# mLSTM decay rows, gate tiles and convolution taps in a new order, and GLA heads in turn, in a two-block float32 kernel

## The reference, cut to what matters

```
h      = rms_norm(x, g) * (1 + sc) + sh              # (512, 1024)
p      = split(h @ w_in)                             # ml_q .. ml_f, gla_q .. gla_a, conf, sc, gate
# mLSTM, 4 heads of 64; with b = cumsum(log_sigmoid(f)) and m the running maximum of (i - b):
qk[t,s] = (q_t . k_s / 8) * exp(i_s - b_s - m_t)     for s <= t, else 0
h_t     = sum_s qk[t,s] v_s / max(|sum_s qk[t,s]|, exp(-(b_t + m_t)))
y_ml    = (head_rms_norm(h_t) * sigmoid(ml_o)) @ w_ml_out
# conformer: 31 causal taps over 256 channels, then layer norm, silu, projection
u      = layer_norm(dwconv31(a * sigmoid(g)));  y_conf = silu(u) @ w_conf_out + b
# GLA, 4 heads of 64, chunks of 16: o = (masked q k) v inside a chunk + q . state before it
merged = g0 * y_ml + g1 * y_gla + g2 * y_conf + g3 * y_sc;   block output = merged @ w_o
```

## Time and profile before

| | |
|---|---|
| median of three executions | 1870.16 us |
| span of the profiled execution, first to last instruction | 1862.2 us |
| what lies around the span (median less span) | 8.0 us |
| mean granted clock of TensorE | 0.944 |
| PE busy | 1752.2 us, 94% |
| DVE / ACT / POOL busy | 900.6 / 662.8 / 421.5 us |
| chain that ended last | PE 81%, DVE 12%, waiting for nothing shown 2%, ACT 2% |

### The profile page before, as it was taken

One profiled execution on the slowest core, in us unless ns is written; L12 is line 12 of the kernel. 1 busy time (PEld: TensorE's weight loads), 2 busy tenths in 40 slices (PEclk: granted clock), 3 DMA queues, 4 the chain that ended last, 5 costly groups with the idle time before them and its releaser, 6 DMA issues.

```text
span 1862.2 us, 20099 instructions
## 1 busy us (share of the span) xinstructions
PE 1752.2 (94%) x7716; PEld 1379.7 (74%) x7716; DVE 900.6 (48%) x1193; ACT 662.8 (36%) x794; POOL 421.5 (23%) x152
## 2 busy tenths in 40 slices
PE   6897999999998979999999799999998999999997
PEld 4676667877877748888888478777767688888886
DVE  4559215332789464444433375385444244444323
ACT  2341215323313254454322432243343355454222
POOL 0347202411433401111100045533203211111000
PEclk8898779977999989999999999999999999999999
DMA  8231202210656213333322122222202233332321
GB/s 291 77 93 46 67 24 68 91 46 23 218 176 216 70 44 100 103 90 90 113 90 91 62 68 91 75 69 70 66 24 68 79 91 90 93 109 90 113 90 45
DMA packets 190956, 168.60 MB, mean 91 GB/s; under 512 B 9157, under 2 KB 180717, under 8 KB 190765
## 3 DMA queue, kind: packets, MB, share of 16 engines
q1 hardware_dynamic: 173485, 148.49, 25.9%
q10 hardware_dynamic: 16800, 16.83, 2.8%
q0 software_dynamic: 608, 2.41, 0.3%
HBM read 165.61 MB, written 2.10 MB: 90 GB/s over the span
## 4 chain that ended last, share of the span: by engine, by line
PE 81%; DVE 12%; issue 2%; ACT 2%; SPq 1%; DMA 1%; POOL 0%; DVEq 0%; ACTq 0%
PE bank L1091 22%; PE bank L1093 22%; PE bank L1092 22%; DVE work L1564 4%; DVE work L1627 2%; PE bank L1173 2%; PE bank L1316 1%; DVE tbuf L1536 1%; PE bank L1116 1%; DVE h_lo L1542 1%; SPq L235 1%; PE bank L1236 1%; PE bank L1449 1%; PE bank L1157 1%; PE bank L1227 1%
## 5 line engine op out<-in xcount | busy, mean ns | idle before, releaser
L1091 PE MATMUL bank<-h_hi,w_hi 128*128 128x512 f32 x1536 | 617.0, 402 | 30.1 <-DVE h_lo L1542 23.9
L1092 PE MATMUL bank<-h_lo,w_hi 128*128 128x512 f32 x1536 | 605.8, 394 | 0.0
L1093 PE MATMUL bank<-h_hi,w_lo 128*128 128x512 f32 x1536 | 605.5, 394 | 0.0
L573 POOL TENSOR_TENSOR w_lo<-w_raw,w_hi 128x2048 fp32r<-128x2048 f32 x63 | 326.1, 5177 | 551.9 <-ACT w_hi L648 551.7
L1091 PEld LDWEIGHTS bank<-h_hi,w_hi 128*128 128x128 f32 x1536 | 293.6, 191 | 114.7 <-issue 35.4
L648 ACT ACTIVATE w_hi<-w_raw 128x2048 fp32r<-128x2048 f32 x131 | 250.3, 1911 | 311.1 <-PE bank L1093 241.0
L1093 PEld LDWEIGHTS bank<-h_hi,w_lo 128*128 128x128 f32 x1536 | 293.2, 191 | 62.6
L1092 PEld LDWEIGHTS bank<-h_lo,w_hi 128*128 128x128 f32 x1536 | 293.9, 191 | 60.5 <-issue 1.7
L1524 DVE TENSOR_TENSOR w_lo<-w_raw,w_hi 128x2048 fp32r<-128x2048 f32 x68 | 156.8, 2306 | 252.5 <-ACT w_hi L648 252.5
L1091 PE MATMUL bank<-y_hi,w_hi 128*128 128x512 f32 x480 | 192.1, 400 | 11.2 <-DVE tbuf L1747 8.4
L1897 DVE SCALAR_TENSOR_TENSOR work<-bank,par,work 128x510 f32<-128x510 f32 (+1 forms) x176 | 123.5, 744 | 142.1 <-ACT work L933 142.1
(11 more groups left out here) (223 smaller groups left out, 1534.4 us busy)
## 6 DMA issues: line engine op xcount, KB each, us to landing
w_raw<-in_w_in SPq DMA_DIRECT2D x94, 512.0 KB, 4.6
w_raw<-in_ffn_w_up SPq DMA_DIRECT2D x44, 512.0 KB, 4.6
w_raw<-in_w_up SPq DMA_DIRECT2D x44, 512.0 KB, 4.6
work<-in_ada_w ACTq DMA_DIRECT2D x16, 1024.0 KB, 7.5
w_raw<-in_ffn_w_down SPq DMA_DIRECT2D x22, 512.0 KB, 4.0
w_raw<-in_w_down SPq DMA_DIRECT2D x22, 512.0 KB, 3.7
work<-in_ada_w SPq DMA_DIRECT2D x8, 1024.0 KB, 12.1
w_raw<-in_w_o SPq DMA_DIRECT2D x8, 512.0 KB, 4.1
```

The costliest lines, as they stand in the source:

```text
L573: pool.tensor_tensor(w_lo[u % 2][:, :], raw[u % 2][:, :], w_hi[u % 2][:, :].bitcast(FP32), ALU.subtract)\
L1091: pe.matmul(dst, w_hi[s][:, at:at + n], hi, start=first, stop=False)
L1092: pe.matmul(dst, w_hi[s][:, at:at + n], lo, start=False, stop=False)
L1093: return pe.matmul(dst, w_lo[s][:, at:at + n], hi, start=False, stop=last)
```

## The change

What it does:

- **Row broadcast once per head.** `ml_spread(h)` spreads -m over all 512 queries once (4 matmuls in place of 16), into bank 3 or 7. DVE adds the mask of all four diagonal blocks in one instruction (`ml_mask`), and the 16 mask matmuls go. ACT now takes the exponential in two instructions, the diagonal block from what DVE wrote and the rest from the bank.
- **Heads in pairs.** The 16 (head, block) pairs become 8 steps; each does the scores of heads h and h + 1 for one block.
- **Gate tiles in halves.** Each step holds one gate3 tile, 12 matmuls and 12 matmuls (`column_part`), with the spread of heads 2 and 3 (step 3) and the outputs of heads 0 and 1 (step 4) between the halves. The gate2 tile in `gla_result` is halved too.
- **Taps.** The conformer's mean moves from ahead of the mLSTM into step 3, its variance into step 5. The taps are spread from before the gate rows to step 2.
- **Low parts.** Those of the four mLSTM units, the four of gate3 and of y3 move from POOL to DVE, between the taps and in steps 0, 2, 4 and 6.
- **Output turn later.** The turn of the mLSTM output moves from ahead of y3 to after the first GLA unit, and what follows it on ACT and DVE too.
- **GLA.** Both heads' scores come first, then half a tile, head 2c within, half a tile, head 2c + 1 within, and `gla_before` alternates the two heads matmul by matmul.
- The value rows have 66 columns per head in place of 65.

The core of the diff (places in `work` and table entries left out):

```diff
-            for u in range(U["gate2"] + 1):
+            for u in range(IFA + 1):
+                lo(u)
+            for u in range(U["y3"] + 1, U["gate2"] + 1):
                 lo(u)
...
+            def ml_decay(h, j, n):
+                g = ml_gt[:, j * MH + h:j * MH + h + 1]
+                if n >= 2:
+                    wait_read(act, T["ml_qk"][n - 2])
+                act.wait_ge(sem("ml_masked"), h + 1)
+                ins = act.activation(tbuf[:, n % 2, 0:P], ml_masked[:, h % 2, j * P:(j + 1) * P], ACT.Exp, bias=g)
+                if j < TT - 1:
+                    ins = act.activation(tbuf[:, n % 2, P:S - j * P], bank[T["ml_d"][h].bank][:, (j + 1) * P:S], ACT.Exp, bias=g)
+                ins.then_inc(sem("ml_exp"), 1)
...
+            def column_part(name, n, k0, k1):
+                u, t, at = U[name] + n // 2, T[name][n], n % 2
+                if k0 == 0:
+                    weights_ready(u)
+                    wait_free(pe, t)
+                for k in range(k0, k1):
+                    mm = three(bank[t.bank][:, :], u, k * 256 + at * P, P, h_hi[:, k, :], h_lo[:, k, :], k == 0, k == KT - 1)
+                if k1 == KT:
+                    done(mm, t)
...
-            for n in range(MH * TT):
-                h, j = divmod(n, TT)
-                if n == CF_VAR_AT:
-                    conformer_mean(T["cf_var"][0], cf_s, sem("cf_sq"))
-                ml_scores(h, j)
-                if h and j == 1:
-                    ml_values(h - 1)
-                if n in GATE3_AFTER:
-                    column_tile("gate3", GATE3_AFTER[n])
-            ml_values(MH - 1)
-            for cc in (6, 7):
-                column_tile("gate3", cc)
+            for h in range(2):
+                ml_spread(h)
+            for step, (h, j) in enumerate(ML_STEPS):
+                if step == CF_MEAN_AT:
+                    conformer_mean(T["cf_mu"][0], cf_acc, sem("cf_conv"))
+                if step == CF_VAR_AT:
+                    conformer_mean(T["cf_var"][0], cf_s, sem("cf_sq"))
+                for hh in range(2):
+                    ml_scores(h + hh, j, 2 * step + hh)
+                column_part("gate3", step, 0, 4)
+                if step == VALUES_AT - 1:
+                    for hh in range(2):
+                        ml_spread(2 + hh)
+                if step == VALUES_AT:
+                    for hh in range(2):
+                        ml_values(hh)
+                column_part("gate3", step, 4, KT)
+            for hh in range(2):
+                ml_values(2 + hh)
...
             def gla_result(c, tile):
                 gla_scores(2 * c)
-                column_tile("gate2", tile)
+                gla_scores(2 * c + 1)
+                column_part("gate2", tile, 0, 4)
                 wait_free(pe, T["gl_o"][c])
                 gla_within(2 * c)
-                gla_scores(2 * c + 1)
-                gla_before(2 * c)
+                column_part("gate2", tile, 4, KT)
                 gla_within(2 * c + 1)
-                done(gla_before(2 * c + 1), T["gl_o"][c])
+                done(gla_before(c), T["gl_o"][c])
...
-            conf_taps(1, TAPS_FIRST)
+            lo(U["ml"])
+            conf_taps(1, 6)
+            lo(U["ml"] + 1)
...
-            conf_taps(TAPS_FIRST, CONF_W)
+            conf_taps(6, 11)
+            lo(U["ml"] + 2)
+            conf_taps(11, 16)
+            lo(U["ml"] + 3)
+            conf_taps(16, 20)
...
+            def ml_mask(h):
+                t = T["ml_d"][h]
+                wait_full(dve, t)
+                if h >= 2:
+                    dve.wait_ge(sem("ml_exp"), 2 * TT - 1 + h % 2)
+                dve.tensor_tensor(ml_masked[:, h % 2, :].rearrange("p (j t) -> p j t", j=TT), bank[t.bank][:, :].rearrange("p (j t) -> p j t", j=TT),
+                                  const("causal_st").unsqueeze(1).broadcast_to([P, TT, P]), ALU.add).then_inc(sem("ml_masked"), 1)
```

More of the change, by code:

```diff
@@ L395, in program @@
         take("gl_z", AUX, MT)
+        take("ml_hT", AUX, MT)
         take("gl_kdT", AUX, MT)
@@ L735, in _ @@
             log_and_exp()
+            split(U["ml"] + 1)
             t = T["ifa"][0]
@@ L794, in _ @@
             act.activation(ml_ms, ml_ms, ACT.Exp, scale=-0.5).then_inc(sem("ml_rs"), 1)
-            for cc in (6, 7):
-                raw_gate("gate3", cc, 3 * KT)
-            open_gates("gate3")
-            split(U["y3"] + 1)
-            act.wait_ge(w_used, U["y3"] + 1)
-            for k in range(2):
-                y_split(ml_q[:, k, :], k, 3 + k)
             u = U["gla"]
@@ L816, in _ @@
             split(u + 2)
+            for k in range(2):
+                y_split(ml_q[:, k, :], k, 3 + k)
+            act.wait_ge(sem("y_lo"), 6)
             for c in range(2):
@@ L1271, in _ @@
                 (token_unit if k == 2 else column_unit)(U["gla"] + k, T["gla"][2 * k:2 * k + 2])
+                if k == 0:
+                    pe.wait_ge(sem("ml_normed"), 1)
+                    for c in range(MT):
+                        turn(T["ml_hT"][c], [(i * P, ml_h[:, i, c * P:(c + 1) * P]) for i in range(TT)])
             for c in range(MT):
@@ L1704, in _ @@
-            ml_divide(MH - 1)
+            for step, (h, j) in enumerate(ML_STEPS):
+                if step == VALUES_AT + 1:
+                    for hh in range(2):
+                        ml_divide(hh)
+                for hh in range(2):
+                    ml_weights(h + hh, j, 2 * step + hh)
+                if step % 2 == 0:
+                    lo(U["gate3"] + step // 2 + 1)
+                if step < CF_MEAN_AT:
+                    conf_taps(25 + 2 * step, 27 + 2 * step)
+                if step == CF_MEAN_AT - 1:
+                    dve.wait_ge(ch.sem, ch.n)
+                    for c in range(2):
+                        dve.nop().then_inc(sem("cf_conv"), 1)
+                if step == CF_MEAN_AT:
+                    conf_center()
+                    for hh in range(2):
+                        ml_mask(2 + hh)
+                if step == CF_VAR_AT + 1:
+                    wait_read(dve, T["cf_var"][0])
+                    for c in range(2):
+                        dve.scalar_tensor_tensor(out=cf_acc[:, c, :], in0=cf_acc[:, c, :], scalar=col("conf_ln_g", c), in1=rstd[:, :],
+                                                 op0=ALU.mult, op1=ALU.mult).then_inc(sem("cf_scaled"), 1)
@@ L1705, in _ @@
+            for hh in range(2):
+                ml_divide(2 + hh)
             for h in range(MH):
@@ L1769, in _ @@
                                   ALU.subtract).then_inc(sem("gl_bs"), 1)
+            for c in range(MT):
+                t = T["ml_hT"][c]
+                wait_full(dve, t)
+                wait_read(dve, T["ml"][6 + c])
+                release(dve.scalar_tensor_tensor(out=ml_q[:, c, :], in0=bank[t.bank][:, :], scalar=col("ml_norm_g", c), in1=ml_o[:, c, :],
+                                                 op0=ALU.mult, op1=ALU.mult), t)
+                wait_read(dve, t)
+                dve.nop().then_inc(sem("y_src"), 1)
+            for k in range(2):
+                y_lo_of(ml_q[:, k, :], k, 5 + k)
             for c in range(2):
```

195 lines of the change are left out of this document (89 added, 106 removed).

## The result

The changed kernel takes **1802.8 us** (median of four executions, 1801.3 to 1804.5), the kernel before in the same comparison 1869.4: a ratio of 0.9641, 95% interval [0.9627, 0.9655], 66.6 us less. The profiled execution has a span of 1801.8 us and a total of 1804.5. The forecast was 1807, the range 1797 to 1828.

The account below looks back on a forecast made before the run. PE was taken to bound the mLSTM stretch, full of small work at mean clock 0.77. 52.3 us saved up to the GLA projections plus 11.1 in the GLA made 63.4 off 1870.2, rounded 1807 us; range 1797 to 1828.

Parts of the forecast that it names:

- Up to the first spread: Stretch before the mLSTM's first spread: DVE's low parts and taps set the pace, first spread issued at 173.8 us.
- From there to y3: First spread to y3 on PE: 68.8 us work, 2.6 waits, 2.5 half clock, together 73.9; y3 starts at 247.7.
- the one of step 5: Second score of step 5 waits 1.0 us for the bank DVE frees at the end of two divides.
- the fifth tile: In y3: 0.4 us lost because DVE frees this tile's bank late, after its divides and squares.
- The GLA: State matmuls with alternating heads at 0.065 us a record, 8.1 us per pair; 11.1 us saved over both pairs.
- The tiny turn at 0.074: Eight tiny matmuls at the mLSTM's turn, 0.074 us each, taken as the dearest that issuing alone can be.
- Sum: Whole kernel: 52.3 us by the GLA projections plus 11.1 in the GLA, 63.4 off the span, 1862.2 to 1798.8.
- The median stands 8.0 above the span, and I keep that: Step from span to time: 1870.2 - 63.4, rounded, gives 1807 us.
- GLA gains nothing: Rival for the GLA heads: a fixed cost per instruction, the 11.1 us fall to about 0, 1818 us; chance 0.20.
- Clock not won back: Rival, first spread to y3: mean clock stays 0.77, 93 us in place of 73.9, 1826 us; chance 0.11.
- DVE becomes the bound: Rival: nine low parts moved to DVE make step 3's mean wait some 20 us, 1827 us; chance 0.08.
- Slower through the weight buffers: Rival: late low parts delay reloads, nine units showing 8.8 us each, 79 us, giving 1886 us; chance 0.02.

Follow-up runs that it names:

- run 3: Changed kernel with the first GLA unit's low part on DVE, after its fourth y3 tile, in place of POOL: 1795.5 us.
- run 5: Changed kernel with the first GLA unit's low part on DVE and, for the second GLA pair, DVE's masked copies ahead of scan and norm: 1788.4 us.
- run 8: Kernel before with the GLA part of the change alone: 1855.3 us against 1867.0, ratio 0.9925.
- run 11: Kernel before, unchanged, profiled again: span 1860.2 us, total 1862.0.
- run 1: Changed kernel with the state matmuls of the two GLA heads one head after the other again: 1814.7 us.
- run 6: Changed kernel with 16 spreads and 16 mask matmuls put back on PE as idle work, overwritten by the scores: 1838.8 us.
- run 7: Changed kernel with the nine low parts of the mLSTM, gate3 and y3 units back on POOL: 1811.1 us.
- run 10: Changed kernel with two idle spreads (4 records, about 1.9 us) on PE ahead of the first spread: 1806.5 us.

## Why the prediction was right, and where it was not

**Up to the first spread.** Forecast 173.8, came at 172.4. DVE's first low part ends at 125.1 as forecast, PE waits 1.7 and not 2.0 for the token unit. The rest is a half-clock stretch of the kernel before in this place (clock 0.97 against 1.00), which I had not counted as a gain.

**From there to y3.** Forecast 73.9, measured 71.5. Spreads 3.8 against 4.4, because two neighbouring ones cost 1.9 together; scores 5.9 against 5.8, so the second head is free as the score rows said; values 0.115 us each at full clock (40 in 4.58) against 0.113; waits 1.8 against 2.6, the one of step 5 did not come; one half-clock stretch, at the values, of two allowed. y3 starts at 243.8 in place of 247.7.

**y3: the step that failed.** I allowed 0.4 us for the fifth tile, "whose bank DVE frees late". It was about 6 (y3 took 17.35 us, against 11.55 in run 3 at full clock): 3.57 of wait and the half clock behind it. The cause, shown by run 3, is POOL's low part of the first GLA unit. It was not among the nine that moved, so I did not follow it; but ACT's split before it is tied to the end of gate3, which now falls together with DVE's last divides. I had named the mutual hold as something that ends and did not ask where the low parts left on POOL would meet DVE next.

**The GLA.** Forecast 11.1, measured 13.4 (8.1 and 5.3). The records came at 7.02 / 124 = 0.0566 us, half of 0.113, and not 0.065: the mis-sized term, 2.1 us over both pairs. The tiny turn at 0.074, which I had taken as a bound, was no guide. PE's wait for the second pair's copy was 4.2 against 3.6; it was DVE's order (run 5). The Trainium skill (TensorE: Matmul & The Clock Gate, "The mechanism") has weight loads overlap a running matmul only where row groups differ; the times fit that, 13.43 us in series and 7.02 in turn. Its other figure, about 62 ns for each matmul ("Wait — 56ns, not 53.3ns?"), is given there for hardware decode off, a condition that the prediction left out. It is above the 56.6 ns a record measured here, but below the 113 ns of a whole matmul of the program, which is two records; so this case doesn't decide on it.

**Sum.** 50.2 at the start of the GLA stage (359.44 and 309.27 us) against 52.3, then 13.4 against 11.1: 63.6 against 63.4. That one miss of 6.0 us (y3) and three of 1.4, 2.4 and 2.3 the other way cancel is luck; the terms show it.

**From span to time.** "The median stands 8.0 above the span, and I keep that" was wrong. In every run here the total lies 1.7 to 2.9 us above that run's own span. The 8.0 compared the span of one execution with the median of others: the profiled execution of before had a total of some 1864 to 1865 (1862.2 + 1.7 to 2.9), below its three timed runs (1868.6 to 1872.6). So the profile of before was a quick one, and the change saves 60 us from profile to profile and 66.6 from median to median. With 2 us around it my span of 1798.8 would have given 1801, 2 us from the measured 1802.8 where 1807 is 4 off.

A possible reason for the quick profile is the hold of run 8, with which the same program is 9.5 us later at the end of the values. Another is where the half clock falls (run 11). In the comparison of run 8 the nine executions of before spread over 14 us (1861.5 to 1875.2), in that of run 11 the seven over 4 (1861.6 to 1865.8), and there the profile had 10.2 us again. The taps of the changed kernel meet no POOL instruction, and its four executions spread over 3. That the hold is the cause of the spread was not shown.

**The rivals.** GLA gains nothing: refuted by run 1. Clock not won back: refuted, 0.98, and run 6 shows that it hangs on the small work on PE. DVE becomes the bound: at the mean one wait of 0.9 us, and run 7 shows the reverse, DVE was later with less to do; but the two longest waits that are left, 3.6 in y3 and 4.2 in the GLA, are both for DVE. Slower through the weight buffers: the waits for low parts are 1.7 and 1.0 us.

What each part is worth, in medians or by the profile: turn-taking 12 to 14 us, low parts on DVE about 8, the mean's place 8, halves 0, and the spreads, masks and pairs 36 to 39 by the reverse experiment. These don't add up exactly, since they share the clock.

## What to carry to other kernels

Count the small float32 matmuls between tiles twice, once for their time and once for the clock that they may cost the tiles (in run 6, 24.3 us and 14.3). When work leaves one of two engines that hold each other, list what stays and look where each piece will now meet the other engine; a short instruction on the path that takes as long as a long one next door is the sign. And compare a profile with its own execution's time, not with the median of others.

## What the runs showed of the hardware

- **DVE and POOL hold each other for whole instructions, either way.** A 0.17 us divide step took 4.60 beside POOL's 4.59 us low part; a low part took 24.00 us beside back-to-back taps in one run and 4.94 in another, where the taps paid. The Trainium skill (SBUF — State Buffer, "SBUF: two separate sides") says that where a DVE instruction with two SBUF inputs meets a POOL instruction that reads SBUF, whichever starts first has the shared ports for the whole instruction. The divide agrees: POOL began at 242.16 us, the step at 242.18, and it ended at 246.77, 0.02 us behind POOL's end. POOL's 24 us are many DVE instructions long, so a run of them keeps POOL out for longer than one.
- **Heads in different rows and columns of the array run side by side down to 16 columns**: 108 to 113 ns a record alone (13.43 us for 124 in run 1, 7.01 for 62 before), 56.6 in turn. In turn the matmuls of the two heads start 6 ns apart and the next two 104 ns on. From start to start a record takes 110 ns alone and 55 in turn, at clock 1.00 and at 0.50 alike.
- **The clock can be at half with PE busy throughout**: 0.83 over 110.1 us with 109.2 busy (run 6), as in the earlier trace rows.
- **Where the half-clock stretches fall changes with a shift of 1.9 us (run 10), and between two profiles of one kernel (run 11).** From the GLA's last mean square on all kernels here have the same program. Its half-clock time, without the last stretch at the end of the span, was 44.4 us (run 11) to 64.9 (the changed kernel), and its length 1398.3 to 1405.9 us, 7.6 us of time. That bounds what two profiles or two medians can tell.
